# Multiplications of a constant table in five waits of TensorE

## The reference, cut to what matters

```python
mod = jax.nn.silu(cvec) @ lw["ada_w"] + lw["ada_b"]
sh1, sc1, g1, sh2, sc2, g2 = [m[:, None, :] for m in jnp.split(mod, ADA_CHUNKS, axis=-1)]
h = _rms_norm(x, lw["norm1_g"]) * (1.0 + sc1) + sh1
mix, new_ctx = _token_mix(h, lw, ctx)
x = x + g1 * mix
h = _rms_norm(x, lw["norm2_g"]) * (1.0 + sc2) + sh2
x = x + g2 * _expert_choice_ffn(h, lw["w_router"], lw["w_expert_gate"],
                                lw["w_expert_up"], lw["w_expert_down"])
...
aff = jax.nn.softmax((h @ w_router).astype(jnp.float32), axis=-1)
gates, idx = lax.top_k(aff.transpose(0, 2, 1), cap)
xs = h[bidx, idx]
```

## Time and profile before

| | |
|---|---|
| three runs | median 2071.69 us, lowest 2068.59, highest 2072.93 |
| profiled execution: own time | 2070.92 us |
| profiled execution: span, first to last instruction | 2069.2 us |
| around the span | 1.7 us |
| TensorE busy | 1771.0 us, 86% of the span |
| VectorE, ScalarE, GpSimd busy | 666.7, 496.2, 154.3 us |
| mean granted TensorE clock | 0.938 of full |
| HBM read, mean rate | 339.39 MB, 166 GB/s |

### The profile page before, as it was taken

How to read it: one execution, slowest core, us unless ns; L and a number is a source line. 1 busy time by engine, 2 the same in 40 slices (tenths; PEclk the granted TensorE clock), 3 DMA queues, 4 the chain that set the end, 5 groups by cost and what they waited for, 6 DMA issues and landing times.

```text
span 2069.2 us, 30757 instructions
## 1 busy us (share of the span) xinstructions
PE 1771.0 (86%) x12119; PEld 1039.6 (50%) x12119; DVE 666.7 (32%) x1306; ACT 496.2 (24%) x1124; POOL 154.3 (7%) x186
## 2 busy tenths in 40 slices
PE   4888998999899778888669799899998995888884
PEld 3557865556555442232255587546565554323222
DVE  1395433221421241222217843414033114212124
ACT  3372441021500201111045515212033003011111
POOL 2004110100000000000100221101000000000000
PEclk9799999999999879999869999999999996999997
DMA  9324411505112409999942324123431143499990
GB/s 333 117 82 165 166 57 41 87 22 167 53 69 110 174 0 368 393 394 394 324 175 82 135 102 145 47 82 46 145 85 41 41 162 122 158 394 394 395 364 31
DMA packets 165633, 344.63 MB, mean 167 GB/s; under 512 B 21130, under 2 KB 23266, under 8 KB 165376
## 3 DMA queue, kind: packets, MB, share of 16 engines
q1 hardware_dynamic: 162560, 338.44, 45.9%
q0 software_dynamic: 2944, 4.39, 1.0%
HBM read 339.39 MB, written 3.41 MB: 166 GB/s over the span
## 4 chain that ended last, share of the span: by engine, by line
PE 71%; DMA 9%; DVE 7%; issue 4%; ACT 4%; DVEq 2%; PEld 1%; ACTq 0%; POOL 0%; SPq 0%; PEldq 0%; POOLq 0%
PE PS L757 19%; DMA arena<-in_w_expert_up_dram 9%; PE PS L1460 8%; PE PS L764 6%; PE PS L1368 4%; PE PS L1327 4%; PE PS L1485 3%; PE PS L729 3%; PE PS L1257 3%; PE PS L1193 2%; PE PS L919 1%; PE PS L805 1%; PE PS L1429 1%; PE PS L911 1%; ACT hT L1550 1%
## 5 line engine op out<-in xcount | busy, mean ns | idle before, releaser
L757 PE MATMUL PS<-hT,ring 128*128 128x384 f32 x1312 | 443.6, 494 | 5.1 <-issue 3.0
L757 PEld LDWEIGHTS PS<-hT,ring 128*128 128x128 f32 x1312 | 250.4, 192 | 183.2 <-issue 20.2
L1460 PE MATMUL PS<-ring,arena 128*48 128x512 f32 x768 | 232.4, 607 | 29.5 <-DMA arena<-in_w_expert_up_dram 16.4
L1514 ACT ACTIVATE arena<-PS 128x512 f32<-128x512 f32 (+3 forms) x246 | 114.1, 497 | 465.3 <-PE PS L729 146.2
L1460 PEld LDWEIGHTS PS<-ring,arena 128*48 128x48 f32 x768 | 69.2, 125 | 186.7 <-issue 163.1
L764 PE MATMUL PS<-ring,hT 128*128 128x256 f32 (+1 forms) x384 | 132.2, 502 | 11.6 <-DVE arena L2105 11.1
L729 PE MATMUL PS<-const,arena 128*128 128x128 f32 (+2 forms) x389 | 55.3, 284 | 71.6 <-DVE arena L2336 35.0
L1460 PE MATMUL PS<-arena 128*48 128x512 f32 x256 | 116.2, 608 | 0.0
L764 PEld LDWEIGHTS PS<-ring,hT 128*128 128x128 f32 x384 | 74.5, 197 | 62.4 <-issue 44.0
L2336 DVE TENSOR_TENSOR arena<-arena,PS 48x512 f32<-48x512 f32 x32 | 22.1, 690 | 237.8 <-ACT arena L1795 237.8
L729 PEld LDWEIGHTS PS<-const,arena 128*128 128x128 f32 (+2 forms) x389 | 44.6, 154 | 104.1 <-issue 68.8
(11 more groups left out here) (326 smaller groups left out, 2262.7 us busy)
## 6 DMA issues: line engine op xcount, KB each, us to landing
ring<-in_w_expert_gate_dram SPq DMA_DIRECT2D x32, 2048.0 KB, 16.0
ring<-in_w_in_dram SPq DMA_DIRECT2D x26, 2048.0 KB, 9.7
ring<-in_ada_w_dram SPq DMA_DIRECT2D x24, 2048.0 KB, 16.8
ring<-in_w_expert_up_dram SPq DMA_DIRECT2D x16, 2048.0 KB, 19.4
ring<-in_w_expert_down_dram SPq DMA_DIRECT2D x16, 2048.0 KB, 18.8
arena<-in_w_expert_up_dram SPq DMA_DIRECT2D x16, 2048.0 KB, 21.6
arena<-in_w_expert_down_dram SPq DMA_DIRECT2D x16, 2048.0 KB, 19.0
ring<-in_w_out_dram SPq DMA_DIRECT2D x4, 2048.0 KB, 7.8
```

The source lines that it names most:

```text
L757: ins = mm(out, w[:, k, 128 * c:128 * c + 128], hT[:, k, :], start=k == 0, stop=k == KT - 1)
L1460: ins = mm(PS[64 * n:64 * n + ROWS, u % 2, :], xs_e[:, u % 2, k, :], expert_view(3 * u + n)[:, k, :], start=k == 0, stop=k == KT - 1)
L1514: return f(out, in_, ACT.Copy)
```

## The change

A helper `keep_clock(n, bank)` is added on TensorE: it multiplies the table of ones with the first 512 columns of `const`, n times, into one bank of PSUM. Nothing reads the result and no semaphore is moved. It is called in each turn of the loop ahead of five waits: 10 times at the layer turn, 6 times ahead of `h0`, 11 times ahead of `h1`, 2 times ahead of `top` and 5 times ahead of `sel`.

```diff
+            def keep_clock(n, bank):
+
+                for _ in range(n):
+                    mm(PS[:, bank, :], ones, const[:, 0:512], start=True, stop=True)
...
             with pe.Fori(0, DEPTH) as l:
                 blk = 0
 
+                keep_clock(10, 3)
                 pe.wait_ge(vec_in, 16 * VEC_LOADS + l * (16 * VEC_LOADS))
 
                 pe.wait_ge(T["exc_dve"].sem, T["exc_dve"].before(l))
...
                 ada_turn(0, 7)
 
+                keep_clock(6, 3)
                 pe.wait_ge(done["nrm_act"], at("nrm_act", l, "h0"))
...
                 square_sum(KT - 1)
+                keep_clock(11, 1)
                 pe.wait_ge(done["nrm_act"], at("nrm_act", l, "h1"))
...
                 hidden_turned(2)
 
+                keep_clock(2, 1)
                 pe.wait_ge(done["rt_dve"], at("rt_dve", l, "top"))
...
                     .then_inc(T["rt_pe"].mark("count"), 1)
+                keep_clock(5, 1)
                 pe.wait_ge(done["rt_dve"], at("rt_dve", l, "sel"))
```

## The result

The changed kernel takes 2081.36 us in the median of 9 runs (2077.03 to 2088.91), against 2071.89 of the kernel before in 9 runs beside them (2068.59 to 2076.14): a ratio of 1.0049, 95% interval 1.0033 to 1.0065, or 9.5 us slower by the medians (10.2 by the ratio). The forecast was 2069.9 us and the range ended at 2077. The profiled execution took 2080.55 us, its span was 2079.0, 9.8 us more than before. In the changed kernel the helper's matmul stands in line 776 and everything behind it moved down by 5 to 10 lines: the sums are line 782, line 825 became 832, line 1382 became 1390, lines 1429 and 1460 became 1439 and 1470.

The account below looks back on a forecast made before the run. TensorE itself was taken to bound most of a layer, its wait for weights the experts. Terms +9.0 + 0 - 2.2 - 2.2 - 6.0 = -1.4 us against 2070.92 gave 2069.5, put at 2069.9 for the median; range 2060 to 2077.

Parts of the forecast that it names:

- Time won or lost ahead of the experts should pass through in full.: Whole kernel: a gain or loss before the experts moves all weight transfers and reaches the end at full size.
- The first norm: Line 825 behind the wait for h0: full clock lasts into it, saving 1.1 us a layer, -2.2 for two.
- The router: Waits for top and sel: counting, transpositions and first gather run faster, -3.0 us a layer, -6.0 for two.
- Layer turn, layer 0: Ten multiplications ahead of the sums: nothing covers them, so they cost +9.0 us, between 7.7 and 17.2.
- Layer turn, layer 1: Ten multiplications in the idle before layer 1: end at 1031, five us early, cost 0, between -1 and +3.
- the forecast's own bounds (3): Turn to layer 1: even at half clock the ten would be late by only 3 us.
- Second norm: Logits of line 1382 behind the wait for h1: 1.1 us saved a layer, between 0 and 5.2, -2.2 for two.
- the third rival: Norms and router: the clock falls again before the waiting work begins; 2077.3 to 2080.3 us, chance 0.19.
- Counting: Router's counting products, 738.17 to 740.52: at full clock 2.3 us become 1.3, -1.0 a layer.
- Transpositions and first gather: Router behind the wait for sel: transpositions -0.8 us and first gather -1.5 us a layer.
- The rule on transposes: Router: transposes don't count as clock work like matmuls, so the two start at half clock; 2073.7 us, chance 0.03.
- the 0.8 named: Forecast's sum: the three runs' median is 0.8 us above the profiled execution, used to move 2069.5 to 2069.9.

Follow-up runs that it names:

- e1: Kernel before plus only the ten multiplications at the layer turn: 1.0064 of before, 13.3 us [9.3, 17.2] slower.
- e2: Kernel before plus the calls ahead of h0, h1, top and sel (6, 11, 2, 5), none at the turn: 5.8 us [2.3, 9.3] faster.
- e7: Kernel before plus six scratch writes on VectorE ahead of its copy of xT, no added matmuls: 7.9 us [5.2, 10.6] slower.
- e13: Kernel before plus eight multiplications ahead of h0 only: nothing measurable at the end, given as +0.4 us [-2.5, 3.1].
- e3: Kernel before plus only the two multiplications ahead of top and five ahead of sel: 1.9 us [-1.0, 5.0] saved at the end.
- e14: Kernel before plus fourteen multiplications ahead of h1 only: 5.0 us [2.7, 7.5] saved at the end.
- e4: Kernel before plus only the six multiplications ahead of h0 and eleven ahead of h1; its own measured time is not in the text.
- e8: Changed kernel with five multiplications at the layer turn instead of ten: 4.1 us faster than the kernel before.

## Why the prediction was wrong

The sum was -1.4 us and +10.2 [6.8, 13.5] were measured. By the parts, the turn cost 13.3 [9.3, 17.2] and not 9.0 (e1), and the other four calls gained 5.8 [2.3, 9.3] and not 10.4 (e2). What is left, some 3 us, is within these intervals.

- **"Time won or lost ahead of the experts should pass through in full."** This is the step that failed. Lost time did (e7: 9.8 us at the first norm, 7.9 at the end). Won time did not at two of three places, since stretches behind it met half clock that they had not met before. The first norm saved more than was forecast (1.8 and 2.2 us against 1.1 each; 4.4 in e13), and nothing measurable of it arrives (e13, +0.4 [-2.5, 3.1]). The router saved what was forecast (7.3 us in this pair of traces, 6.1 in the mean of all, against 6.0), and the experts took 1.6 us a layer of it back; e3 has 1.9 [-1.0, 5.0] at the end. Time won at the second norm did arrive (e14).
- **Layer turn, layer 0, +9.0.** Right place, right price: +10.1 at the vectors, +8.9 at the first norm (63.31 against 54.45). The ten met half clock for 3.4 us inside.
- **Layer turn, layer 1, 0, "ends at 1031, five us ahead".** Wrong: I started the ten when TensorE came free. They start 3.0 to 5.0 us later, behind the loop's branch, and take 10.3 to 10.9. In the changed kernel 0.76 us were left, in e1 it was late by 1.6, in the forecast's own bounds (3).
- **Second norm, -2.2.** Mis-sized: the logits took 10.28 and 10.42 us. The clock fell 0.3 us into them, behind 3.04 us of idle, near to what the third rival had; at 0.46 us of rest the same row took 7.66 (e14). That rival ("the clock is down again before the waiting work begins", 0.19, 2077.3 to 2080.3) came nearest, with the wrong place for most of the loss: line 832 and the counting products did begin at full clock.
- **Router, item by item.** Counting -1.0 forecast: 7.78 to 7.21 and 7.80 to 6.75 us with what surrounds it, -0.6 and -1.1. Transpositions and first gather -2.3 forecast: -2.4 and -2.3. Right. The rule on transposes weighed there has no sign here either: the clock rose at 741.35, among the transpositions and ahead of the two. Whether these transpositions, two MATMUL rows each against the identity, are of the kind that the rule is about, no run shows.
- **Readings that were off.** The clock had fallen at 24.84 not after 3.9 us of pure idle: TensorE turned the vectors at 23.25 (0.33 us). The fall at the second norm came at 707.5 and not at 707.76. And 0.4 us, not the 0.8 named, were added for the median. None of these carries the miss.

The sum with the measured sizes: turn +10.5 by places (8.9, and 1.6 as in e1), first norm 0, second norm -0.2, router -7.3, experts +3.2: +6.2 us. By e1 the turn is +13.3, which makes +9.0, and with the router's mean of all traces (-6.1) +10.2, closer to the measured time than the intervals warrant. The step from 10.5 to 13.3 is within e1's interval, but e8 says that the ten cost more than their place; of what that consists stays open.

## What to carry to other kernels

Fill a wait only where the filling ends ahead of it even when it starts late and meets half clock, and fill it nearly to its end: 3.0 us of rest gave 0.0 to 0.4 us at the logits, 0.46 us gave 2.7. At the first norm 2.7 us of rest left 1.8 to 2.3 us of saving in five of eight layers and none in three (e4 and layer 0 of e8), 0.96 us left 1.6 to 4.2 in all twelve. Count a gain of clock only when it has been seen at the end of the kernel, since what follows a shortened stretch may meet half clock where it met none (first norm: 2.2 us a layer saved, 0 arrived).

## What the runs showed of the hardware

- TensorE did not start dense, dependency-free work at the turn of its loop until 3.04, 4.92 and 5.03 us after its last product, in three traces; the profile calls it issue.
- Full busyness and full clock did not go together: in the changed kernel TensorE was busy in all of 65.41 to 75.64 (rows of 32 columns, then of 384) and in 13.03 of the 13.65 us from 727.65 (mostly rows of 16 and 128), and both ran at 0.50. At line 939 in e13 the clock fell behind 3.10 us of which TensorE was busy for 2.58.
- A matmul of the table costs some 0.44 us a row at full clock (20 rows in 8.82 us at layer 0 of e1), and the ten with 3.4 us at half clock inside took 10.52.
